# Zero products on TensorE around the root norms, and a joint first unit with four weight places in the gated stages

## The reference, cut to what matters

```
h = adaln(x, norm_g[i, s], shift, scale)            # root norm, gain, shift
x = x + 0.5 * gate * swiglu(h, ffn_w_in, ffn_w_out)  # 1024 -> 2 x 2816 -> 1024
```

## Time and profile before

| what | value |
|---|---|
| median of 3 runs | 3371.5 us (3364.65 to 3376.15) |
| profiled execution, first to last instruction (its span; no other time of it is given) | 3367.9 us |
| PE busy | 3090.6 us, 92% |
| PEld (weight load) busy | 2753.4 us, 82% |
| DVE busy | 2435.7 us, 72% |
| ACT busy | 1680.4 us, 50% |

### The profile page before, as it was taken

How to read it: one execution, slowest core, us unless ns; L and a number is a source line. 1 busy time by engine, 2 the same in 40 slices (tenths; PEclk the granted TensorE clock), 3 DMA queues, 4 the chain that set the end, 5 groups by cost and what they waited for, 6 DMA issues and landing times. The chain is left out here.

```text
span 3367.9 us, 58567 instructions
## 1 busy us (share of the span) xinstructions
PE 3090.6 (92%) x23849; PEld 2753.4 (82%) x23849; DVE 2435.7 (72%) x3648; ACT 1680.4 (50%) x2444; POOL 134.1 (4%) x152
## 2 busy tenths in 40 slices
PE   7679999899888899999987999999899998988899
PEld 6577777689887789898976899899689898978798
DVE  6669999778765468787577587785668788674555
ACT  4437777654552354544553445544554545442444
POOL 0010000100102000000000000000000000011000
PEclk8779999999999799999986999999899999998899
DMA  9347999767410267586430386774057687300442
GB/s 383 141 175 295 370 369 366 292 244 307 188 69 4 78 253 307 225 312 262 162 128 1 119 312 262 265 307 193 11 225 306 231 310 272 123 2 3 160 183 83
DMA packets 77517, 698.67 MB, mean 207 GB/s; under 512 B 8432, under 2 KB 12528, under 8 KB 55408
## 3 DMA queue, kind: packets, MB, share of 16 engines
q1 hardware_dynamic: 30928, 525.65, 39.7%
q10 hardware_dynamic: 42912, 157.31, 12.3%
q0 software_dynamic: 3456, 12.58, 1.0%
HBM read 691.31 MB, written 4.19 MB: 207 GB/s over the span
## 5 line engine op out<-in xcount | busy, mean ns | idle before, releaser
L1074 PE MATMUL banks<-u_split,w_split 128*128 128x512 f32 x2816 | 1014.9, 403 | 22.9 <-DVE u_split L1319 21.0
L1143 ACT ACTIVATE w_split<-ring 128x1024 fp32r<-128x1024 f32 x513 | 541.3, 1058 | 672.1 <-PE banks L1075 406.5
L1250 DVE TENSOR_TENSOR w_split<-ring,w_split 128x1024 fp32r<-128x1024 f32 x513 | 625.5, 1222 | 293.3 <-ACT w_split L1143 288.7
L1075 PE MATMUL banks<-u_split,w_split 128*128 128x256 f32 x2816 | 797.3, 283 | 0.0
L1074 PEld LDWEIGHTS banks<-u_split,w_split 128*128 128x128 f32 x2816 | 537.3, 191 | 158.8 <-issue 17.9
L1075 PEld LDWEIGHTS banks<-u_split,w_split 128*128 128x128 f32 x2816 | 539.7, 192 | 0.0
L1066 PE MATMUL banks<-h_split,w_split 128*128 128x256 f32 x1408 | 400.6, 285 | 7.9 <-DVE w_split L1250 7.9
L1067 PE MATMUL banks<-h_split,w_split 128*128 128x256 f32 x1408 | 400.5, 284 | 0.0
L1068 PE MATMUL banks<-h_split,w_split 128*128 128x256 f32 x1408 | 400.4, 284 | 0.0
L520 PE MATMUL banks<-bufs_split,ring_split 128*128 128x256 f32 x1376 | 397.0, 289 | 0.0
L584 DVE CUSTOM_DVE_ANT_0 bufs<-bufs 128x1024 f32<-128x1024 f32 x300 | 357.0, 1224 | 12.7 <-DVE w_split L1250 12.7
(11 more groups left out here) (489 smaller groups left out, 4931.5 us busy)
## 6 DMA issues: line engine op xcount, KB each, us to landing
ring<-stream SPq DMA_DIRECT2D x155, 3072.0 KB, 10.9
bufs<-ada ACTq DMA_DIRECT2D x296, 512.0 KB, 10.4
bufs<-ada POOLq DMA_DIRECT2D x23, 512.0 KB, 6.7
bufs<-ada SPq DMA_DIRECT2D x3, 2048.0 KB, 16.1
ring<-stream SPq DMA_DIRECT2D x2, 2688.0 KB, 10.0
bufs<-c_rows SPq DMA_DIRECT2D x9, 512.0 KB, 4.3
ring<-stream SPq DMA_DIRECT2D x1, 2704.0 KB, 13.1
ring<-stream SPq DMA_DIRECT2D x1, 2176.0 KB, 8.9
```

The lines of the kernel that those rows point to most:

```text
L1074: pe.matmul(bank.rearrange("p (a t) -> p a t", a=2), w_high, u_split[:, k, :, :], start=(k == 0), stop=False, skip_group_check=True)
L1075: return pe.matmul(bank[:, 0:SEQ], w_low, u_split[:, k, 0, :], start=False, stop=(k == KC - 1), skip_group_check=True)
L1143: nc.scalar.activation(w_split[:, slot, 0, :], piece(j, b), ACT.Copy).then_inc(high.sem, 1)
L1250: e = nc.vector.tensor_tensor(w_split[:, slot, 1, :], piece(j, b), w_split[:, slot, 0, :].bitcast(F32), ALU.subtract)
```

## The change

- `keep_busy` runs n products of zeros with 512 columns into a bank that nothing reads. In `paired_sums` one stands behind each of the first five steps, four stand between the sums and the wait for the inverse root, three behind `spread_tokens`, in the eleven places named above. Six more stand at the head of `first_up_products`, in all eight gated stages.
- In the first unit of a gated stage, blocks 0, 1 and 2 run side by side for each chunk where three pieces are there early; else blocks 0 and 1 for the first five chunks, and from the sixth on all three, with block 2's first five chunks made up as soon as the sixth chunk is there.
- Piece 3 gets its own place, in `w_spare` and in the second half of buffer 9, and its high part no longer waits for `piece_used` 1.

```diff
--- before.py
+++ after.py
@@ -747,7 +747,13 @@
     last.then_inc(summed.sem, summed.count(1))
 
 
-def paired_sums(core, pe, squares, bank, paired, squared, summed):
+def keep_busy(core, pe, bank, n):
+
+    for _ in range(n):
+        pe.matmul(core.psum[:, bank, :], core.zeros[:, 0:P], core.zeros[:], start=True, stop=True)
+
+
+def paired_sums(core, pe, squares, bank, paired, squared, summed, idle_bank=None):
 
     ones = core.const("ones")[:, 0:1]
     for c in (0, 4, 2, 5, 6, 7):
@@ -757,6 +763,8 @@
             pe.wait_ge(squared.sem, squared.at(c + 1))
         for t in range(2):
             last = pe.matmul(core.psum[:, bank + t, 0:1], squares[:, c, t * P:(t + 1) * P], ones, start=(c == 0), stop=(c == KC - 1))
+        if idle_bank and c < KC - 1:
+            keep_busy(core, pe, idle_bank, 1)
     last.then_inc(summed.sem, summed.count(1))
 
 
@@ -819,7 +827,8 @@
 
 
 
-    def __init__(self, core, kind, squares, bank, eps=NORM_EPS, turn=0):
+    def __init__(self, core, kind, squares, bank, eps=NORM_EPS, turn=0, idle_bank=None):
+        self.idle_bank = idle_bank
         self.core, self.kind, self.squares, self.bank, self.eps, self.turn = core, kind, squares, bank, eps, turn
         self.ready, self.squared, self.summed, self.spread = (core.event(n) for n in ("x_ready", "x_squared", "x_summed", "x_spread"))
         self.paired = core.event("x_paired")
@@ -834,9 +843,13 @@
             sums_everywhere(core, pe, core.x, self.bank, self.ready, self.summed)
         else:
             inverse = core.event("inverse")
-            paired_sums(core, pe, self.squares, self.bank, self.paired, self.squared, self.summed)
+            paired_sums(core, pe, self.squares, self.bank, self.paired, self.squared, self.summed, self.idle_bank)
+            if self.idle_bank:
+                keep_busy(core, pe, self.idle_bank, 4)
             pe.wait_ge(inverse.sem, inverse.at(self.turn + 1))
             spread_tokens(core, pe, 2, ROOT_BANK, self.spread)
+            if self.idle_bank:
+                keep_busy(core, pe, self.idle_bank, 3)
 
     def square(self, act, c):
         act.wait_ge(self.ready.sem, self.ready.at(c + 1))
@@ -1005,7 +1018,7 @@
     b_sum = work[:, 1536:2048].rearrange("p (f t) -> p f t", t=SEQ)
     y = core.psum[:, 4:8, :].rearrange("p b (c t) -> p (b c) t", t=SEQ)
     u_split, w_split, h_split = core.u_split, core.w_split, core.h_split
-    after = NextNorm(core, then, core.buf(6), 0) if then else None
+    after = NextNorm(core, then, core.buf(6), 0, idle_bank=2) if then else None
     next_early = 2 if next_key else 0
     with nc.Block() as block:
         y_done = core.event("glu_down_done")
@@ -1026,6 +1039,12 @@
         assert ranges == 2 * ada_turns + odd and (not odd or rest)
         column0 = range0 * KC
 
+        fourth = (core.w_spare[:], core.bufs_split[:, 9, D:2 * D])
+
+        def w_part(slot, part):
+
+            return fourth[part] if slot == "fourth" else w_split[:, slot, part, :]
+
         def sums(which, part):
             return core.psum[:, 2 * which:2 * which + 2, part * SEQ:(part + 1) * SEQ]
 
@@ -1070,7 +1089,7 @@
             def up_block(b, slot, k):
 
                 bank = core.psum[:, b, :]
-                w_high, w_low = (w_split[:, slot, part, k * P:(k + 1) * P] for part in range(2))
+                w_high, w_low = (w_part(slot, part)[:, k * P:(k + 1) * P] for part in range(2))
                 pe.matmul(bank.rearrange("p (a t) -> p a t", a=2), w_high, u_split[:, k, :, :], start=(k == 0), stop=False, skip_group_check=True)
                 return pe.matmul(bank[:, 0:SEQ], w_low, u_split[:, k, 0, :], start=False, stop=(k == KC - 1), skip_group_check=True)
 
@@ -1088,19 +1107,24 @@
 
             def first_up_products():
 
-                for b in range(2):
+                blocks_of = [list(range(3))] * KC if early >= 3 else [[0, 1]] * 5 + [[0, 1, 2]] * 3
+                keep_busy(core, pe, 2, 6)
+                for b in blocks_of[0]:
                     pe.wait_ge(low.sem, low.at(b + 1))
                 for k in range(KC):
                     pe.wait_ge(u_low.sem, u_low.at(k + 1))
-                    for b in range(2):
+                    if k and blocks_of[k] != blocks_of[k - 1]:
+                        pe.wait_ge(low.sem, low.at(3))
+                        for earlier in range(k):
+                            up_block(2, 2, earlier)
+                    for b in blocks_of[k]:
                         last = up_block(b, b, k)
                         if k == KC - 1:
                             last.then_inc(piece_used.sem, 1)
-                for b in range(2, 4):
-                    pe.wait_ge(low.sem, low.at(b + 1))
-                    for k in range(KC):
-                        last = up_block(b, b % 3, k)
-                    last.then_inc(piece_used.sem, 1)
+                pe.wait_ge(low.sem, low.at(4))
+                for k in range(KC):
+                    last = up_block(3, "fourth", k)
+                last.then_inc(piece_used.sem, 1)
 
             def down_products(j, at, last_unit=False):
 
@@ -1136,11 +1160,11 @@
         @block.scalar
         def _(act):
             def high_part(j, b, number, slot):
-                if isinstance(number, int) and number < 3:
+                if isinstance(number, int) and number < 4:
                     pass
                 else:
                     act.wait_ge(piece_used.sem, piece_used.at(number - 2))
-                nc.scalar.activation(w_split[:, slot, 0, :], piece(j, b), ACT.Copy).then_inc(high.sem, 1)
+                nc.scalar.activation(w_part(slot, 0), piece(j, b), ACT.Copy).then_inc(high.sem, 1)
 
             def loaded(j, at):
                 act.wait_ge(core.loaded[(unit0 + j) % SLOTS].sem, 16 * ((unit0 + j) // SLOTS + 1) + (at - j) * (16 // SLOTS))
@@ -1204,7 +1228,7 @@
                     act.activation(u_split[:, c, 0, :], src[:, c, :], ACT.Copy).then_inc(u_high.sem, u_high.count(1))
                 if c == 3 and early < 3:
                     high_part(0, 2, 2, 2)
-            high_part(0, 3, 3, 0)
+            high_part(0, 3, 3, "fourth")
             copy_a(0, 0)
             if ranges:
                 act.wait_ge(c_loaded.sem, c_loaded.at(16))
@@ -1247,7 +1271,7 @@
         def _(dve):
             def low_part(j, b, number, slot):
                 dve.wait_ge(high.sem, high.at(number + 1))
-                e = nc.vector.tensor_tensor(w_split[:, slot, 1, :], piece(j, b), w_split[:, slot, 0, :].bitcast(F32), ALU.subtract)
+                e = nc.vector.tensor_tensor(w_part(slot, 1), piece(j, b), w_part(slot, 0).bitcast(F32), ALU.subtract)
                 e.then_inc(low.sem, 1)
 
             def sum_a(j, at):
@@ -1333,7 +1357,7 @@
                 if c == 5 and early < 3:
                     low_part(0, 2, 2, 2)
             u_low_part(KC - 1)
-            low_part(0, 3, 3, 0)
+            low_part(0, 3, 3, "fourth")
             sum_a(0, 0)
             if ranges:
                 dve.wait_ge(c_ready.sem, c_ready.at(1))
@@ -1788,7 +1812,7 @@
 
 
     y = core.psum[:, 0:4, :].rearrange("p b (c t) -> p (b c) t", t=SEQ)
-    after = NextNorm(core, "root", core.buf(9), 4)
+    after = NextNorm(core, "root", core.buf(9), 4, idle_bank=6)
     w_split = core.w_split
     next_early = 3 if next_key else 0
     next_unit = core.place[(next_key, 0)][0] if next_key else 0
```

## The result

| | before | changed |
|---|---|---|
| median | 3368.55 us (3364.65 to 3376.15, 4 runs) | 3407.28 us (3402.03 to 3412.32, 4 runs) |
| profiled execution: span | 3367.9 us | 3410.2 us |
| TensorE's mean granted clock in it | 0.931 | 0.938 |

The ratio is 1.0114 [1.0096, 1.0131]: the changed kernel is 38.7 us slower. 3398 was forecast, 9 us less. The direction and the range held, near the range's upper end (+42), and the sum of +26.9 fell short by 12 us. TensorE's clock is a little higher and the kernel slower: the two do not go together here.

A forecast was written before the change was run, and what follows sets the result against it. TensorE was taken to bound the stages, a single-file path the boundaries. Terms 12.1 + 1.1 + 7.7 - 2.4 - 1.2 + 5.6 + 4 = 26.9 us over 3367.9; 3398 us on the median, range +10 to +42.

The forecast's parts named there:

- Zeros among the sums: Five zero products ahead of the last sum at eleven boundaries, hardly hidden by waits: 1.1 us each, 12.1 us slower.
- Four and three zeros: At the boundaries: four ahead of the spread nearly covered, 1.1 us in all; three behind it uncovered, 7.7 us.
- The lower level on the zeros: Clock still falls at some boundaries, onto zeros on the path: three of 1.3 us, 4 us; bounds 0 and 19.
- Spread back: Six of eleven spreads ran at the lower level; with the clock held, 6 x 0.4 = 2.4 us come back.
- Six at the head: Gated stage's head: 1.4 us inside TensorE's 1.75 us wait, costing nothing; at the lower level 2.6 us, 0.8 too many.
- Joint unit, early 3: First unit of three stages: `copy_a` shifts +0.15 and -0.95, about -0.4 in the last stage; -1.2 us in all.
- Joint unit, early 0 or 2: First unit of five stages: `copy_a` 1.6 us late, partly absorbed in four (1.0 each); 5.6 us slower in all.
- the gap ahead of unit 1: Sign of being right: a gap of 2 us between the clearing zeros and unit 1; no cost was given.
- A: Rival for the whole kernel: clock held and zeros find cover, -9 or -11 us, 3361 us; chance 0.05.
- B: Rival, no difference: clock gains 14 us in long stages, zeros cost as computed, +4.5 us, 3376 us; chance 0.10.
- C: Rival: zeros do not lift the clock; everything but the sums runs at 0.50, near 3415 us; chance 0.10.
- D: Rival: products of zeros might not count as work for the clock; treated as C, no chance of its own.

The follow-up runs named there:

- z_only: The change with all its zero products but the first unit as it was before; +27.8 us over the kernel before, ratio 1.0082.
- head_only: The change with only the six zero products at each gated stage's head, none around the norm; +13.2 us over the kernel before, ratio 1.0044.
- unit_only: The kernel before with the joint first unit and piece 3's own place, no added zero products; +19.8 us, ratio 1.0056.
- dense: The change with three zero products instead of one behind each of the first five sum steps; +48.4 us over the kernel before, ratio 1.0139.
- no_three: The change without the three zero products behind the spread; +29.7 us over the kernel before, ratio 1.0089.

## Why the prediction was right, and where it fell short

- **Zeros among the sums, right.** 12.1 forecast; 10.5 by taking them out. The sums took 4.0 us at the two places where the clock held, as the forecast's first sign says.
- **Four and three zeros.** 1.1 and 7.7 forecast, about 6 and 9.0 measured. At a place where the clock held all twelve cost 1.40 us net of the faster spread: +1.16 to the start of the last sum, +0.19 from there to the spread, -0.47 in it, +0.52 behind it. Eleven such places are 15.4, where 12.1 + 1.1 + 7.7 - 2.4 = 18.5 was forecast. Where the clock fell, the four and the three cost 1.1 and 1.25 at most places, by these same starts.
- **The lower level on the zeros: named, and far too small.** The text said "nearest to that row I take three boundaries of 1.3: 4 us". It was nine boundaries of (37.0 - 2 x 1.40) / 9 - 1.40 = 2.4 us in the profiled execution: 21.6 us, above the upper bound of 19 that stood beside it. The mechanism was right, its size was not. The row showed one stretch, and the lower level often lasted for two (1196.8 to 1203.5 above). `z_only`'s four of eleven says that the count differs between executions. By medians the term is smaller: the change and `head_only` differ by 25.5 us for the twelve zeros (29.4 by their profiles), which leaves 25.5 - 15.4 = 10, and about 15 if one adds the 5.4 us by which the six at the head push the first products in `head_only` and not in the change. Both are estimates.
- **Spread back, -2.4: too much.** From its first product to its last the spread is 0.47 us shorter at the two places where the clock held. At the nine others it ran at the lower level. Over all eleven it is 0.9 us.
- **Six at the head, 0: right in the change**, where the first product follows the root's first row by the same 1.75 us. "At the lower level 2.6 us, 0.8 too many" is what `head_only` shows.
- **Joint unit, early 3.** `copy_a` forecast at +0.15 and -0.95 (22 x 0.35 + 0.5 is 8.2, not the 8.15 written there); measured +0.38 and -0.85. The -0.4 of the last stage counts `sum_a`'s place in the queue too: there `copy_a` came 0.38 later and unit 1 0.25 sooner.
- **Joint unit, early 0 or 2.** `copy_a` forecast at +1.6; measured +1.69, +1.78, +1.80, +1.71 and +1.42. That part of it is absorbed in the four stages with odd `ranges` held too: unit 1's second block ended 1.24, 1.15 and 1.02 us late in three of them, against 1.0. In the fourth, ffn20, where the clock fell onto unit 1, it was 2.8.
- **What was missed: the gap ahead of unit 1.** The text gave "a gap of 2 us between the clearing zeros and unit 1" as a sign of being right, and did not ask what the clock makes of it. It fell there in three stages, for about 1.5 us each, and these 4.5 us are most of the 7.0 by which the gated stages' +11.4 exceed the forecast of +4.4. In `unit_only`, with no zeros at the head, filling the gap gave 12.9 by medians.
- **The rivals.** A: the clock was up at the first products in all eight stages, as A said and as the first half of the sign against the forecast; but its other half did not come (unit 1 came 0.4 to 1.8 us later in six stages, and in the two others at most 0.86 sooner), and the zeros found no cover. A's gain of 14 us is some 4 (`z_only`). B needed that gain and falls with it. C and D fall by `dense`, where zeros held the clock at every place. C's 3415 was also too low by its own terms: 11 x (0.9 + 0.6) + 8 x 0.8 + 2.4 + 3 x 1.6 = 30 us over a sum without the 4, which is near 3424.
- **The total.** The terms made 26.9 us, the runs 38.7. What is missing is in two terms, the lower level on the zeros (4 against 10 or more) and the gap (0 against 4.5). The range held because its upper end had been set by the first of them, at 19.

## What to carry to other kernels

Here filler products paid only in a wait that somebody else ends. Ahead of a reduction that all engines wait for, or of a stage's end that drains the queue, each costs its length (0.23 us at 512 columns), and if the clock falls there anyway, nearly twice that (0.43). Ask of each stretch at the lower level whether its products are on the path at all: here the three stages whose first unit TensorE bounds gained 4 us from the clock, and the five whose rows come from VectorE nothing. And when an order is made tighter, look at where TensorE comes to stand for longer: the new gap can drop the clock for the products behind it. A few zeros in that gap were the cheap cure: they took back 12.9 of the joint unit's 19.8 us.

## What had not been expected of the hardware

- With five single zero products among the one-column products the clock fell at 9, 4 and 11 of 11 places in one execution each of three kernels (the change, `z_only`, `no_three`); with fifteen it held at 11 of 11 (`dense`), through the spread and the stage's end behind it. A place cost 3.4 us in the change and 3.9 in `dense` on average in the profiles, though ten zero products more are 2.3 us at 0.23 each.
- A gap of 1.87 us on TensorE, in a stretch with 1.53 busy of 3.40 us, was followed by a stretch at 0.50 (`unit_only`, ffn10). With gaps of 1.7 to 1.9 us in all eight stages of that execution this came in four and not in the others.
- The same instructions gave times more than 10 us apart: 35 executions of the kernel before took 3360.7 us (mean granted clock 0.933) to 3377.6 us (0.928). Code that no edit touched lay up to 17.5 us from its time in another profile. One profile cannot size a term of this kind.
